# Sums of squares as a rounded part and a remainder, multiplied by ones inside the third column

## The chip, the cores and the metric

The kernel runs on one core of a Trainium2 chip. The metric is the time of one execution on the device in microseconds (us). Engines are named as in the profile: PE is the matmul engine (PEld its weight loads), ACT is ScalarE, DVE is VectorE, POOL is GpSimd, SP issues most transfers.

## The reference

One inference step of a decoder of two layers on 320 tokens (256 of a prompt, 8 x 8 of a batch with a cache), with a width of 1024, all in fp32. Each layer has three sub-layers, and each of them begins with an RMS norm over the width:

```python
def rmsnorm(x, gain):
    xf = x.astype(jnp.float32)
    y = xf * lax.rsqrt(jnp.mean(xf * xf, axis=-1, keepdims=True) + RMS_EPS)
    return (y * gain.astype(jnp.float32)).astype(x.dtype)

x = x + 0.5 * swiglu(rmsnorm(x, ffn1_norm), ffn1_w_gate, ffn1_w_up, ffn1_w_down)
z = rmsnorm(x, mix_norm) @ w_in          # then attention, pooling, convolution, gating
x = x + jnp.concatenate([att, pool, conv, gmlp], axis=-1) @ w_out
x = x + 0.5 * swiglu(rmsnorm(x, ffn2_norm), ffn2_w_gate, ffn2_w_up, ffn2_w_down)
```

The keys, values and states of the mixers are returned too.

## The kernel before

Tokens lie along the free axis (320 columns), features on the 128 partitions. Every large matrix product is made of fp32r matmuls: weights and inputs are each split into a rounded part ("hi") and a remainder ("lo"), and a product is hi x hi + hi x lo + lo x hi, three matmuls for each tile of 128 x 128 weights. The weights stream in through four slots (`raw`, `w_hi`, `w_lo`, index j): SP loads a slot, ACT rounds it (`round_slot`, L971 to L977), POOL subtracts (`split_iteration`, L494 to L501), PE multiplies. In the stages whose input is a norm, a slot is one output column of eight k tiles, 24 matmuls, and its result goes to bank j; an iteration is four columns. Loading waits for the split of the slot's last content, rounding for the transfer (`raw_in`) and for PE to be done with the slot (`slots`), and PE waits for the split (`split`) and for the bank (`taken`).

The norm is applied behind the product: the input enters the product multiplied by its gain alone (`xg_hi`, `xg_lo`), and DVE multiplies what it reads out of a bank by `rms`, the reciprocal of the root of the mean square. The squares are added up on ACT and DVE while the sub-layer before ends (`norm_input`, `add_square`), last into `sumsq`. Then

- PE multiplies `sumsq` by a matrix of ones in fp32 (`sum_squares`, L644 to L647, called at L642 for the first norm of the first layer, behind column 2, and at L677 for the others, ahead of column 2), into bank 6;
- ACT takes the root into `root` (`root_of_norm`, L956 to L958);
- DVE takes the reciprocal into `rms` (`invert_norm`, L1229 to L1232), and only then can read out the banks 0 to 3 of the first iteration (L1241, L1243, L1283), which PE needs free for the next.

All engines work through their own program in order, written out by hand. What stands on ACT around the root decides what waits with it: at the first norm of a layer (`first_step`, L994 to L1005) two slots of the next iteration are rounded ahead of the root and one behind it; at the second (L1076, L1077) the root comes right behind the last squares, and two slots follow; at the third (L1192) four copies of states (L1195, L1197) and a table load follow, and then the slots.

SP, between layers, issues seven small loads (`load_small`, L367 to L377) ahead of the slots of the first stage's second iteration.

Of the kernel before, what the change touches and what calls it, by code (L numbers as in the profile page):

```python
# [24 lines left out]
F32 = mybir.dt.float32  # L25
F32R = mybir.dt.float32r
I32 = mybir.dt.int32
ALU = mybir.AluOpType
ACT = mybir.ActivationFunctionType
AX = mybir.AxisListType  # L30

P = 128
DEPTH, D_MODEL, FFN = 2, 1024, 2816
SEQ, DEC_B, DEC_T = 256, 8, 8
NS = DEC_B * DEC_T
TOK = SEQ + NS
# [5 lines left out]
RMS_EPS, LN_EPS = 1e-6, 1e-5  # L42
SCALE = HEAD ** -0.5
DT = D_MODEL // P
# [55 lines left out]
def hybrid_decoder(nc, xT, w8, w11, gains, vecs, consts, pool_w, conv_pw, sp_wT, sp_b,  # L100
# [3 lines left out]
    with ctx:  # L104
        place = [16512]

        def sb(name, shape, dt=F32, at=None):
            n = 4
            for s in shape[1:]:
                n *= s  # L110
            offset = place[0] if at is None else at[0]
            t = nc.alloc_sbuf_tensor_at(name, shape, dt, offset=offset)
            end = offset + (n + 31) // 32 * 32
            if at is None:
                place[0] = end
                assert end <= 229344, (name, end)
            else:
                at[0] = end
                assert end <= at[1], (name, end, at[1])
            return t  # L120
# [14 lines left out]
        h_lo = sb("h_lo", [P, FT, TOK], F32R)  # L135
        ffn_region[1] = place[0]
        cst = sb("cst", [P, NC_])
        ones = sb("ones", [P, P])
        gain = sb("gain", [P, (3 * DEPTH + 1) * DT])
        vec = sb("vec", [P, DEPTH * NV])  # L140
        page_row = sb("page_row", [1, DEC_B * PAGES], I32)
# [6 lines left out]
        pool_in = sb("pool_in", [P, GT, POOL_HIST + SEQ + DEC_B * (POOL_HIST + DEC_T)])  # L148
        conv_y = sb("conv_y", [P, GT, TOK])
        rms = sb("rms", [P, TOK])  # L150
        root = sb("root", [P, TOK])
        sumsq = sb("sumsq", [P, TOK])
        square = sb("square", [P, 2, TOK])
        tmp = sb("tmp", [P, 8, TOK])
        q_pad = sb("q_pad", [P, GT, DEC_B, 32])
# [58 lines left out]
        def sig(name, per_layer, head=0):  # L214
            return Signal(ctx.enter_context(nc.semaphore(name)), per_layer, head)
# [21 lines left out]
        squared_first = sig("squared_first", 0)  # L237
        squared_too = sig("squared_too", 0)
        summed = sig("summed", 3 * DT, DT)
        norm_sum = sig("norm_sum", 3)  # L240
        norm_root = sig("norm_root", 3)
        norm_ok = sig("norm_ok", 3)
# [102 lines left out]
        def hold(engine, sem, value):  # L345


            engine.wait_ge(sem, value)
            engine.sem_inc(passed.sem, 1)
# [246 lines left out]
        def _(pe):  # L596
# [46 lines left out]

            def sum_squares(L, n):  # L644

                pe.wait_ge(summed.sem, L * summed.per + (n + 1) * DT)
                pe.matmul(bank[6][:, 0:TOK], ones[:, :], sumsq[:, :], start=True, stop=True).then_inc(norm_sum.sem, 1)  # L647

            def column(L, base, tile0, i, j):

                bank_free(L, i * 4 + (tile0 + j))
                use_slot(L, base, i, j, bank[j][:, 0:TOK], range(8), xg_hi, xg_lo, True, True)
# [5 lines left out]
            def open_columns(L, base, tile0, norm):  # L658

                def products(j, k):  # L660
                    hi, lo = w_hi[:, j, k * P:(k + 1) * P], w_lo[:, j, k * P:(k + 1) * P]
                    out = bank[j][:, 0:TOK]
                    pe.matmul(out, hi, xg_hi[:, k, :], start=k == 0, stop=False, skip_group_check=True)  # L663
                    pe.matmul(out, hi, xg_lo[:, k, :], start=False, stop=False, skip_group_check=True)  # L664
                    return pe.matmul(out, lo, xg_hi[:, k, :], start=False, stop=k == DT - 1, skip_group_check=True)  # L665

                for j in range(2):
                    bank_free(L, tile0 + j)
                    pe.wait_ge(split.sem, split.at(L, base * 4 + j + 1))
                    for k in range(DT - 1):  # L670
                        if j == 0:
                            pe.wait_ge(xg_lo_ok.sem, xg_lo_ok.at(L, norm * DT + k + 1 - DT))
                        products(j, k)
                pe.wait_ge(xg_lo_ok.sem, xg_lo_ok.at(L, norm * DT))
                for j in range(2):
                    products(j, DT - 1).then_inc(slots.sem, 1)
                sum_squares(L, norm)  # L677
                for j in range(2, 4):
                    column(L, base, tile0, 0, j)

            def down(L, base, tile0, ffn):
                with pe.Fori(0, IT_D // 2) as i2:
# [83 lines left out]
            def conv_mean(L):  # L766
                pe.wait_ge(taps.sem, taps.at(L, taps.per))
                pe.wait_ge(late_taps.sem, late_taps.at(L, late_taps.per))
                for c in range(GT):
                    mm = pe.matmul(bank[7][:, 0:TOK], ones[:, :], conv_y[:, c, :], start=c == 0, stop=c == 1)  # L770
                mm.then_inc(cv_mean.sem, 1)

            def conv_variance(L):
                pe.wait_ge(cv_sq.sem, cv_sq.at(L, 2))
                for c in range(GT):
                    mm = pe.matmul(bank[7][:, 0:TOK], ones[:, :], conv_sq[:, c, :], start=c == 0, stop=c == 1)
                mm.then_inc(cv_var.sem, 1)

            def prompt_attention_transposes(L):
# [173 lines left out]
        def _(act):  # L953
            act.sem_inc(states_out.sem, 16)

            def root_of_norm(L, n):  # L956
                act.wait_ge(norm_sum.sem, norm_sum.at(L, n + 1))
                act.activation(root[:, :], bank[6][:, 0:TOK], ACT.Sqrt, bias=eps_rms, scale=1.0 / D_MODEL).then_inc(norm_root.sem, 1)  # L958

            def round_input(gain_col, d):  # L960

# [9 lines left out]
            def round_slot(L, base, i, j, halves):  # L971

                count = halves[j][1]
                act.wait_ge(raw_in[j].sem, L * raw_in[j].per + (base + i) * 16 + 16)

                act.wait_ge(slots.sem, L * slots.per + (base + i) * 4 + j + 1)
                act.activation(w_hi[:, j, 0:count * P], raw[:, j, 0:count * P], ACT.Copy).then_inc(split_hi.sem, 1)  # L977
# [16 lines left out]
            def first_step(L):  # L994

                round_slot(L, BASE_G1, 1, 0, HALVES8)
                round_slot(L, BASE_G1, 1, 1, HALVES8)
                root_of_norm(L, 0)
                round_slot(L, BASE_G1, 1, 2, HALVES8)
                act.preload_act_table(ACT.Silu)  # L1000
                silu(L, 0, 0, T_G1)
                round_slot(L, BASE_G1, 1, 3, HALVES8)
                round_h(L, 0, 0, 0)
                silu(L, 0, 1, T_G1)
                round_h(L, 0, 1, 0)  # L1005
# [15 lines left out]
            def norm_tile(L, tile0, norm, d, e):  # L1021
                hold(act, taken.sem, L * taken.per + d + (tile0 + 1 + taken.head))
                norm_input(L * (3 * DT) + d + norm * DT, d, e, L * summed.per + d + (norm * DT - 1))

            def down(L, base, tile0, norm, last):

                def step(i, e):
                    for j in range(4):
                        round_slot(L, base, i + 1, j, HALVES11)
                    norm_tile(L, tile0, norm, i, e)  # L1030

                act.preload_act_table(ACT.Sqrt)
                with act.Fori(0, DT // 2 - 1) as i2:
                    for e in range(2):
                        step(i2 * 2 + e, e)
                step(DT - 2, 0)
                for j in range(4):
                    if last:
                        round_slot(L + 1, BASE_G1, 0, j, HALVES8)
                    else:  # L1040
                        round_slot(L, BASE_I, 0, j, HALVES8)
                norm_tile(L, tile0, norm, DT - 1, 1)
# [30 lines left out]
            with act.Fori(0, DEPTH) as L:  # L1073
                first_step(L)
                gate_up(L, BASE_G1, T_G1, 0, 1)
                down(L, BASE_D1, T_D1, 1, False)  # L1076
                root_of_norm(L, 1)  # L1077

                def sigmoid(c):
# [107 lines left out]
                for i in range(IT_O):  # L1187
                    for j in range(4):
                        base_next, i_next = ((BASE_O, 1), (BASE_G2, 0))[i]
                        round_slot(L, base_next, i_next, j, HALVES8)  # L1190
                        norm_tile(L, T_O, 2, 4 * i + j, j % 2)
                root_of_norm(L, 2)  # L1192
                for c in range(GT):
                    _, rows = split_tokens(conv_in[:, c, :], CONV_HIST + DEC_T, CONV_HIST)
# [7 lines left out]
        @block.vector  # L1202
        def _(dve):
            dve.sem_inc(taken.sem, 4)
            for n, (ap, value) in enumerate(((stat[:, 42:43], 1.0), (stat[:, 60:61], RMS_EPS), (stat[:, 61:62], LN_EPS), (ones[:, :], 1.0), (q_pad[:, :, :, :], 0.0),
                                             (conv_in[:, :, 0:CONV_HIST], 0.0), (pool_in[:, :, 0:POOL_HIST], 0.0))):
                last = dve.memset(ap, value)
            last.then_inc(filled.sem, 1)
# [18 lines left out]
                    dve.tensor_tensor(sumsq[:, :] if d == DT - 1 else square_sum, square_sum, squares, ALU.add).then_inc(summed.sem, 1)  # L1227

            def invert_norm(L, n):  # L1229
                dve.wait_ge(norm_root.sem, norm_root.at(L, n + 1))  # L1230
                dve.reciprocal(rms[:, :], root[:, :]).then_inc(norm_ok.sem, 1)
                hold(dve, norm_ok.sem, norm_ok.at(L, n + 1))  # L1232

            def gate_up_step(L, base, tile0, ffn, i):
# [401 lines left out]
```

## Time and profile before

| | us |
|---|---|
| time, median of 3 | 1172.51 (1172.4 to 1175.3) |
| the profiled execution | 1173.95 |
| its span | 1172.1 |
| PE busy in it | 1152.9 (98%) |
| POOL busy | 815.1 (70%) |
| DVE busy | 635.4 (54%) |
| ACT busy | 545.5 (47%) |

The profile is of one execution. Times in its rows count from the span's start. A row of the order in time begins with the start and the length in us; "x8" stands for eight instructions in a row, and a bracket tells how long the engine had been idle and what released it. Matmuls overlap, so the length of one is more than the distance to the next.

### The profile page before, as it was taken

The numbers are of one execution on the slowest core, as the hardware profiler recorded it, in microseconds if no ns is written. First come the engines' busy times: TensorE is split into PE (matmuls) and PEld (weight loads), VectorE is DVE, ScalarE is ACT, GpSimd is POOL, SyncE is SP. The second block draws the span as 40 slices with busy tenths as digits, with TensorE's granted clock in tenths as the row PEclk, the third lists the DMA queues.
The fourth block names the chain that finished last, engine by engine and source line by source line (L and its number), as shares of the span: only waits on it lengthen the run. The fifth ranks groups of instructions, "written<-read, shape, count | busy, mean of one in ns | idle before, by whom it ended". The sixth has DMA issues, their size and how long they took to land.

```text
span 1172.1 us, 23918 instructions
## 1 busy us (share of the span) xinstructions
PE 1152.9 (98%) x7912; PEld 1132.8 (97%) x7912; DVE 635.4 (54%) x894; ACT 545.5 (47%) x822; POOL 815.1 (70%) x425
## 2 busy tenths in 40 slices
PE   7999999999999999999999999999999999999998
PEld 6999999998899999999999999999987999999998
DVE  5777762249856544432247776622597664444222
ACT  5444444444665444444444444444357654444444
POOL 5776667777766766667767777677686776666677
PEclk9999999999999999999999999999999999999999
DMA  8454435556535544445564444455563654444455
GB/s 289 154 161 145 154 107 151 147 177 192 173 112 165 176 144 154 140 122 148 169 183 161 144 145 150 122 148 168 179 183 121 173 156 153 156 148 125 138 150 170
DMA packets 72795, 183.14 MB, mean 156 GB/s; under 512 B 10274, under 2 KB 25890, under 8 KB 72738
## 3 DMA queue, kind: packets, MB, share of 16 engines
q1 hardware_dynamic: 72256, 181.33, 50.8%
q10 hardware_dynamic: 482, 1.16, 0.3%
q8 instruction: 23, 0.38, 0.1%
q14 instruction: 34, 0.28, 0.1%
HBM read 178.88 MB, written 3.58 MB: 156 GB/s over the span
## 4 chain that ended last, share of the span: by engine, by line
PE 45%; POOL 25%; issue 24%; DVE 2%; DMA 1%; POOLq 1%; SPq 1%; DVEq 1%; ACT 0%; ACTq 0%
POOL w_lo L500 24%; PE bank L604 13%; PE bank L605 13%; PE bank L607 13%; DVE bank L1292 1%; PE bank L886 1%; PE bank L888 1%; PE bank L887 1%; POOL win L532 1%; DMA x<-in_xT 1%; DMA raw<-in_w 1%; PE bank L664 0%; PE bank L665 0%; PE bank L663 0%; POOLq L499 0%
## 5 line engine op out<-in xcount | busy, mean ns | idle before, releaser
L500 POOL TENSOR_TENSOR w_lo<-raw,w_hi 128x1024 fp32r<-128x1024 f32 (+2 forms) x355 | 776.0, 2192 | 331.2 <-ACT w_hi L977 330.9
L977 ACT ACTIVATE w_hi<-raw 128x1024 fp32r<-128x1024 f32 (+2 forms) x355 | 340.6, 961 | 410.1 <-PE bank L607 388.2
L604 PE MATMUL bank<-xg_hi,w_hi 128*128 128x320 f32 x1552 | 482.2, 311 | 4.0 <-DVE tmp L1241 2.0
L607 PE MATMUL bank<-xg_hi,w_lo 128*128 128x320 f32 x1552 | 479.5, 309 | 0.0
L605 PE MATMUL bank<-xg_lo,w_hi 128*128 128x320 f32 x1552 | 479.5, 309 | 0.0
L604 PEld LDWEIGHTS bank<-xg_hi,w_hi 128*128 128x128 f32 x1552 | 291.3, 188 | 8.0 <-issue 4.6
L605 PEld LDWEIGHTS bank<-xg_lo,w_hi 128*128 128x128 f32 x1552 | 291.3, 188 | 0.4
L607 PEld LDWEIGHTS bank<-xg_hi,w_lo 128*128 128x128 f32 x1552 | 291.3, 188 | 0.0
L604 PE MATMUL bank<-h_hi,w_hi 128*128 128x320 f32 x704 | 217.5, 309 | 0.0
L605 PE MATMUL bank<-h_lo,w_hi 128*128 128x320 f32 x704 | 217.5, 309 | 0.0
L607 PE MATMUL bank<-h_hi,w_lo 128*128 128x320 f32 x704 | 217.5, 309 | 0.0
L1248 DVE TENSOR_TENSOR h_lo<-tmp,h_hi 128x320 f32 (+1 forms) x88 | 169.8, 1930 | 73.4 <-ACT h_hi L991 73.4
L1265 DVE SCALAR_TENSOR_TENSOR x<-bank,x 128x320 f32<-128x320 f32 x48 | 23.4, 486 | 201.1 <-PE bank L607 198.6
L604 PEld LDWEIGHTS bank<-h_hi,w_hi 128*128 128x128 f32 x704 | 132.1, 188 | 0.0
L605 PEld LDWEIGHTS bank<-h_lo,w_hi 128*128 128x128 f32 x704 | 132.1, 188 | 0.0
L607 PEld LDWEIGHTS bank<-h_hi,w_lo 128*128 128x128 f32 x704 | 132.1, 188 | 0.0
L1243 DVE TENSOR_TENSOR tmp<-bank,rms 128x320 f32<-128x320 f32 x88 | 42.9, 487 | 130.4 <-PE bank L607 130.2
L1215 DVE SCALAR_TENSOR_TENSOR xg_lo<-x,gain,xg_hi 128x320 fp32r<-128x320 f32 x56 | 72.3, 1299 | 56.8 <-ACT xg_hi L962 56.8
L987 ACT ACTIVATE tmp<-tmp 128x320 f32<-128x320 f32 x88 | 40.9, 465 | 91.9 <-DVE tmp L1241 91.7
L1246 DVE TENSOR_TENSOR tmp<-tmp 128x320 f32<-128x320 f32 x88 | 62.2, 707 | 9.5 <-ACT tmp L987 7.2
L1320 DVE SCALAR_TENSOR_TENSOR conv_y<-conv_in,vec,conv_y 128x64 f32<-128x64 f32 x88 | 62.7, 753 | 2.8
L991 ACT ACTIVATE h_hi<-tmp 128x320 f32 (+1 forms) x88 | 41.2, 469 | 28.9 <-DVE tmp L1246 28.9
(187 smaller groups left out, 846.2 us busy)
## 6 DMA issues: line engine op xcount, KB each, us to landing
raw<-in_w SPq DMA_DIRECT2D x227, 512.0 KB, 3.9
raw<-in_w SPq DMA_DIRECT2D x64, 384.0 KB, 3.1
raw<-in_w SPq DMA_DIRECT2D x64, 320.0 KB, 2.9
k_all<-in_cache_kT SPq DMA_DIRECT2D x32, 128.0 KB, 3.1
v_past<-in_cache_v SPq DMA_DIRECT2D x32, 128.0 KB, 2.8
cst<-in_consts ACTq DMA_DIRECT2D x1, 997.0 KB
out_yT<-x SPq DMA_DIRECT2D x1, 960.0 KB, 5.9
x<-in_xT SPq DMA_DIRECT2D x2, 320.0 KB, 4.0
```

The source lines that it names most:

```text
L500: pool.tensor_tensor(w_lo[:, j, 0:count * P], raw[:, j, 0:count * P], w_hi[:, j, 0:count * P].bitcast(F32), ALU.subtract).then_inc(split.s ...
L604: pe.matmul(out, hi, in_hi[:, k, :], start=first and n == 0, stop=False)
L605: pe.matmul(out, hi, in_lo[:, k, :], start=False, stop=False)
L607: mm = pe.matmul(out, lo, in_hi[:, k, :], start=False, stop=last and end)
L977: act.activation(w_hi[:, j, 0:count * P], raw[:, j, 0:count * P], ACT.Copy).then_inc(split_hi.sem, 1)
L987: act.activation(tmp[:, 2 + m, :], tmp[:, m, :], ACT.Silu).then_inc(silu_ok.sem, 1)
L991: act.activation(h_hi[:, bass.ds(i * 2 + m, 1), :].rearrange("p a t -> p (a t)"), tmp[:, 6 + m, :], ACT.Copy).then_inc(h_hi_ok.sem, 1)
L1215: dve.scalar_tensor_tensor(out=xg_lo[:, bass.ds(d, 1), :].rearrange("p a t -> p (a t)"), in0=one, scalar=gain[:, bass.ds(gain_col, 1)], in ...
L1243: dve.tensor_tensor(tmp[:, 4 + m, :], bank[2 * m + 1][:, 0:TOK], rms[:, :], ALU.mult).then_inc(taken.sem, 1)
L1246: dve.tensor_tensor(tmp[:, 6 + m, :], tmp[:, 2 + m, :], tmp[:, 4 + m, :], ALU.mult).then_inc(h_ok.sem, 1)
L1248: dve.tensor_tensor(h_lo[:, bass.ds(i * 2 + m, 1), :].rearrange("p a t -> p (a t)"), tmp[:, 6 + m, :], h_hi[:, bass.ds(i * 2 + m, 1), :].b ...
L1320: dve.scalar_tensor_tensor(out=y, in0=window, scalar=weight, in1=y, op0=ALU.mult, op1=ALU.add).then_inc(batch_taps.sem, 1)
```

## The change

The matrix of ones becomes fp32r (the same bytes are still read as fp32 by the convolution's two sums). ACT rounds `sumsq` into `sum_hi` (`round_sum`, right ahead of each root), DVE subtracts to give `sum_lo` (at the head of `invert_norm`), and PE multiplies both by the ones, in two fp32r matmuls into bank 6, after a wait for the remainder. In `open_columns` this moves from ahead of column 2 to the middle of it, behind its fourth k tile; in `first_columns` its place stays. The root is written over the sum in bank 6, and the reciprocal reads it there.

```diff
@@ allocation, signals
-        ones = sb("ones", [P, P])
+        ones_r = sb("ones_r", [P, P], F32R)
+        ones = ones_r[:, :].bitcast(F32)
-        root = sb("root", [P, TOK])
+        sum_hi = sb("sum_hi", [P, TOK], F32R)
+        sum_lo = sb("sum_lo", [P, TOK], F32R)
+        sum_hi_ok = sig("sum_hi_ok", 3)
+        sum_lo_ok = sig("sum_lo_ok", 3)
@@ PE
             def sum_squares(L, n):
-                pe.wait_ge(summed.sem, L * summed.per + (n + 1) * DT)
-                pe.matmul(bank[6][:, 0:TOK], ones[:, :], sumsq[:, :], start=True, stop=True).then_inc(norm_sum.sem, 1)
+                pe.wait_ge(sum_lo_ok.sem, sum_lo_ok.at(L, n + 1))
+                pe.matmul(bank[6][:, 0:TOK], ones_r[:, :], sum_hi[:, :], start=True, stop=False, skip_group_check=True)
+                pe.matmul(bank[6][:, 0:TOK], ones_r[:, :], sum_lo[:, :], start=False, stop=True, skip_group_check=True).then_inc(norm_sum.sem, 1)
@@ PE, open_columns
-                sum_squares(L, norm)
-                for j in range(2, 4):
-                    column(L, base, tile0, 0, j)
+                bank_free(L, tile0 + 2)
+                pe.wait_ge(split.sem, split.at(L, base * 4 + 3))
+                for k in range(DT):
+                    if k == DT // 2:
+                        sum_squares(L, norm)
+                    mm = products(2, k)
+                mm.then_inc(slots.sem, 1)
+                column(L, base, tile0, 0, 3)
@@ ACT
+            def round_sum(L, n):
+                hold(act, summed.sem, L * summed.per + (n + 1) * DT)
+                act.activation(sum_hi[:, :], sumsq[:, :], ACT.Copy).then_inc(sum_hi_ok.sem, 1)
...
-                act.activation(root[:, :], bank[6][:, 0:TOK], ACT.Sqrt, bias=eps_rms, scale=1.0 / D_MODEL).then_inc(norm_root.sem, 1)
+                act.activation(bank[6][:, 0:TOK], bank[6][:, 0:TOK], ACT.Sqrt, bias=eps_rms, scale=1.0 / D_MODEL).then_inc(norm_root.sem, 1)
...
                 round_slot(L, BASE_G1, 1, 0, HALVES8)
                 round_slot(L, BASE_G1, 1, 1, HALVES8)
+                round_sum(L, 0)
                 root_of_norm(L, 0)
...
+                round_sum(L, 1)
                 root_of_norm(L, 1)
...
+                round_sum(L, 2)
                 root_of_norm(L, 2)
@@ DVE
             def invert_norm(L, n):
+                dve.wait_ge(sum_hi_ok.sem, sum_hi_ok.at(L, n + 1))
+                dve.tensor_tensor(sum_lo[:, :], sumsq[:, :], sum_hi[:, :].bitcast(F32), ALU.subtract).then_inc(sum_lo_ok.sem, 1)
                 dve.wait_ge(norm_root.sem, norm_root.at(L, n + 1))
-                dve.reciprocal(rms[:, :], root[:, :]).then_inc(norm_ok.sem, 1)
+                dve.reciprocal(rms[:, :], bank[6][:, 0:TOK]).then_inc(norm_ok.sem, 1)
```

## Rows read from the trace of the kernel before

**Rows 1.** The page: busy us, share of the span and instructions of each engine.

```profile
PE 1152.9 (98%) x7912; PEld 1132.8 (97%) x7912; DVE 635.4 (54%) x894; ACT 545.5 (47%) x822; POOL 815.1 (70%) x425
```

**Rows 2.** Order in time around the first norm: start, length, engine, instruction, count, idle before.

```profile
17.11 1.34 PE L625 MATMUL bank<-xg_lo,w_hi 128*128 128x320 f32 x8
22.98 0.70 PE L647 MATMUL bank<-sumsq,ones 128*128 128x320 f32 x2
23.01 1.06 ACT L977 ACTIVATE w_hi<-raw 128x1024 fp32r<-128x1024 f32 x1 [3.18 <-DMA raw<-in_w]
23.97 0.51 ACT L958 ACTIVATE root<-bank,stat 128x320 f32<-128x320 f32 x1
24.37 2.41 POOL L500 TENSOR_TENSOR w_lo<-raw,w_hi 128x1024 fp32r<-128x1024 f32 x1
24.51 2.15 DVE L1231 RECIPROCAL rms<-root 128x320 f32<-128x320 f32 x1 [4.46 <-ACT root L958]
24.68 1.34 PE L625 MATMUL bank<-xg_lo,w_hi 128*128 128x320 f32 x8
27.54 0.41 PE L604 MATMUL bank<-xg_hi,w_hi 128*128 128x320 f32 x1 [0.34 <-DVE tmp L1241]
```

**Rows 3.** DVE's subtractions (line L1248: ns min/median/max), and one beside POOL in time.

```profile
L1248 DVE TENSOR_TENSOR h_lo<-tmp,h_hi x88: 492/2028/2326, 30.1 to 1091.7; 128x320 f32 x84, 128x320 fp32r<-128x320 f32 x4
...
606.94 2.58 POOL L500 TENSOR_TENSOR w_lo<-raw,w_hi 128x1024 fp32r<-128x1024 f32 x1
607.87 2.00 DVE L1248 TENSOR_TENSOR h_lo<-tmp,h_hi 128x320 fp32r<-128x320 f32 x1 [0.62 <-ACT h_hi L991]
```

**Rows 4.** Order in time around the first norm of the second layer.

```profile
596.18 0.70 PE L647 MATMUL bank<-sumsq,ones 128*128 128x320 f32 x2
601.03 1.06 ACT L977 ACTIVATE w_hi<-raw 128x1024 fp32r<-128x1024 f32 x1 [2.18 <-DMA raw<-in_w]
601.99 0.51 ACT L958 ACTIVATE root<-bank,stat 128x320 f32<-128x320 f32 x1
602.16 2.40 POOL L500 TENSOR_TENSOR w_lo<-raw,w_hi 128x1024 fp32r<-128x1024 f32 x1 [0.83 <-ACT w_hi L977]
605.55 0.41 PE L604 MATMUL bank<-xg_hi,w_hi 128*128 128x320 f32 x1 [1.62 <-DVE tmp L1241]
```

**Rows 5.** Order in time around the second norm of the first layer.

```profile
250.24 0.48 DVE L1227 TENSOR_TENSOR sumsq<-bank,square 128x320 f32<-128x320 f32 x1
252.91 0.70 PE L647 MATMUL bank<-sumsq,ones 128*128 128x320 f32 x2
253.65 0.53 ACT L958 ACTIVATE root<-bank,stat 128x320 f32<-128x320 f32 x1 [5.71 <-PE bank L647]
255.20 2.42 POOL L500 TENSOR_TENSOR w_lo<-raw,w_hi 128x1024 fp32r<-128x1024 f32 x1 [5.23 <-ACT w_hi L977]
```

**Rows 6.** Order in time behind the third norm of the first layer.

```profile
366.89 1.06 ACT L977 ACTIVATE w_hi<-raw 128x1024 fp32r<-128x1024 f32 x1
368.03 2.42 POOL L500 TENSOR_TENSOR w_lo<-raw,w_hi 128x1024 fp32r<-128x1024 f32 x1 [7.99 <-ACT w_hi L977]
370.90 0.31 PE L604 MATMUL bank<-xg_hi,w_hi 128*128 128x320 f32 x1
```

**Rows 7.** PE's first matmuls in order of time.

```profile
8.64 1.27 PE L625 MATMUL bank<-xg_lo,w_hi 128*128 128x320 f32 x4
9.71 1.27 PE L629 MATMUL bank<-xg_hi,w_lo 128*128 128x320 f32 x4
11.47 1.99 PE L621 MATMUL bank<-xg_hi,w_hi 128*128 128x320 f32 x4 [0.49 <-ACT xg_hi L962]
15.39 1.88 PE L621 MATMUL bank<-xg_hi,w_hi 128*128 128x320 f32 x8
```

**Rows 8.** Stretches: length, busy us (instructions) by engine, granted clock, DMA share, GB/s.

```profile
0.00:6.50 6.50, 0.00 (x0) 0.01 (x1) 1.89 (x9) 2.93 (x4) 0.25 (x5) 1.00 0.62 168
6.50:16.60 10.10, 9.22 (x29) 7.78 (x30) 5.96 (x11) 7.84 (x14) 4.58 (x3) 1.00 1.03 385
```

More of the change, by code:

```diff
@@ L769, in conv_mean @@
                 for c in range(GT):
-                    mm = pe.matmul(bank[7][:, 0:TOK], ones[:, :], conv_y[:, c, :], start=c == 0, stop=c == 1)
+                    mm = pe.matmul(bank[7][:, 0:TOK], ones, conv_y[:, c, :], start=c == 0, stop=c == 1)
                 mm.then_inc(cv_mean.sem, 1)
@@ L775, in conv_variance @@
                 for c in range(GT):
-                    mm = pe.matmul(bank[7][:, 0:TOK], ones[:, :], conv_sq[:, c, :], start=c == 0, stop=c == 1)
+                    mm = pe.matmul(bank[7][:, 0:TOK], ones, conv_sq[:, c, :], start=c == 0, stop=c == 1)
                 mm.then_inc(cv_var.sem, 1)
@@ L1204, in _ @@
             dve.sem_inc(taken.sem, 4)
-            for n, (ap, value) in enumerate(((stat[:, 42:43], 1.0), (stat[:, 60:61], RMS_EPS), (stat[:, 61:62], LN_EPS), (ones[:, :], 1.0), (q_pad[:, :, :, :], 0.0),
+            for n, (ap, value) in enumerate(((stat[:, 42:43], 1.0), (stat[:, 60:61], RMS_EPS), (stat[:, 61:62], LN_EPS), (ones, 1.0), (q_pad[:, :, :, :], 0.0),
                                              (conv_in[:, :, 0:CONV_HIST], 0.0), (pool_in[:, :, 0:POOL_HIST], 0.0))):
```

## Prediction

> **What bounds the kernel now.** I read the busy table first: the matmul engine (PE) is busy 98% of the span, the next engine (POOL) 70% [rows 1]. A kernel like this ends later by each gap that opens in the PE stream, and earlier by each matmul taken out of it; work elsewhere counts only where it makes PE wait. So I looked at PE's own order in time, around the six sums of squares (three norms in each of two layers), and beside it at what ScalarE (ACT), VectorE (DVE) and POOL do there. The unit of all that follows is the distance of two matmul starts, 128x128 on 320 columns: from 17.11 us, the second third of column 1, to the sum at 22.98 there are 40 of them (16 left of column 1, 24 of column 2), so 5.87/40 = 0.147 us each [rows 2]. A column is 24 of them, 3.52 us.
>
> **What the change takes away.** A sum is two records [rows 2]. From its start at 22.98 to the second third of the next column at 24.68 lie 1.70 us, of which eight matmuls are 1.18, so the fp32 sum costs PE 0.52 us [rows 2]. Two fp32r matmuls of the same shape cost 0.29. The change takes 0.23 us from PE at each norm, 1.4 us in all. The trace shows no fp32r matmul against a constant matrix; the kernel's other fp32r matmuls are the nearest rows. If the pair still ran like fp32, a sum would cost 1.04 and the six norms 3.1 us more than now instead of 1.4 less.
>
> **What it adds.** Ahead of the pair stand a copy on ACT (128x320, about 0.47 us, like the root's 0.51) and a subtraction on DVE with both operands in SBUF. The same kind of subtraction in this kernel takes 0.49 us when POOL is idle, but 2.03 at the median [rows 3]: the one at 607.87 ended at 609.87, 0.35 us after the POOL subtraction that ran from 606.94 to 609.52 [rows 3]. I take from this that it lands 0.35 us after the end of the POOL instruction that it finds running, and 0.49 after its start where POOL is idle. PE now waits for its result, and all that is queued on PE behind that wait (the rest of the third column, the fourth, and what follows) waits with it. The root comes after the pair: before, it began 0.74 us after the sum's start (252.91 to 253.65) [rows 5]; the pair is 0.24 shorter, so 0.50. The root in PSUM and the reciprocal that reads it there are in no row; DVE's and ACT's rows with an operand in PSUM (0.51 for the root, which reads it) bound them to some 0.1 us either way, and I take nothing.
>
> **First norm, layer 0: +3.7 us.** This sum stands after the whole third column, the change doesn't move it. PE arrives at 22.98 [rows 2]. But ACT, in the order of its program, rounds slot 1 of the next iteration before it comes to the new copy, and that waits for a weight transfer until 23.01; the root, next in line, began at 23.97 [rows 2]. The copy takes that place: 23.97 to 24.44. The subtraction reaches DVE at 24.48, 0.11 us after a POOL instruction began, 24.37 to 26.78 [rows 2], and lands at 27.13. PE starts the pair at S = 27.2, idle for 4.1 us. Now the chain behind: the root at S + 0.50, the reciprocal 0.54 later (23.97 to 24.51), and the next iteration's first column, for which bank 0 must be read out, 3.03 later (24.51 to 27.54) [rows 2]: 31.27. PE itself, with 26 matmuls, is done at S + 3.82 = 31.0, so the bank is last. It was 27.54: +3.7.
>
> **First norm, layer 1: +5.0 us.** Here the pair stands after the fourth of the eight k tiles of column 2. Without the sum that now lies at 596.18, PE gets there at 596.18 + 12 x 0.147 = 597.94. ACT again has two slots to round first; the second waits 2.18 us for its transfer and starts at 601.03, the root behind it at 601.99 [rows 4]. Nothing of this hurt before: PE had the sum done long ago and two columns to go. Now the copy takes the root's place, 601.99 to 602.46; POOL begins its subtraction at 602.16 and ends at 604.56 [rows 4], so the remainder lands at 604.91 and S = 604.98. PE idles 7.0 us. After it come 2 + 12 + 24 matmuls, 5.59 us, to 610.57; the chain through the root would allow 609.05, and slots 0 and 1 have both been split by 604.56, so nothing else is late. It was 605.55, with 1.62 us of idle before it that the new stall swallows [rows 4]: +5.0.
>
> **Second norm, both layers: -0.5 us.** The sum of squares starts at 250.24 and takes 0.48, ACT and DVE then stand idle and POOL does until 255.20 [rows 5]; the copy and the remainder are done by 251.9. PE comes at 252.91 + 1.76 = 254.67 and doesn't wait. The root slides by 1.76 - 0.24 = 1.52 us, and with it POOL's first split of the next iteration, to 256.72 to 259.14. It is needed after 50 matmuls, at 260.2, so it stays covered by 1.1 us. The saving stands: 2 x 0.23.
>
> **Third norm, both layers: +2.4 us.** Again PE doesn't wait for the remainder, and again ACT slides by 1.52 us. But here it has four copies and a table load between root and slot: rounding starts at 366.89, POOL runs from 368.03 to 370.45, and PE takes the slot at 370.90 [rows 6], a cover of 0.45 us only. POOL will end at 371.97, and PE, 0.1 us later, start at 372.1: +1.2 in each layer. The bounds are -0.23 (all covered) and +1.5 (the whole slide). The slots behind have a column, 3.52 us, each against 2.42 on POOL, and catch up.
>
> **Sum at full matmul rate:** 3.7 + 5.0 - 0.5 + 2.4 = 10.6 us.
>
> **What the idle does to the matmul rate.** In the first 16 us matmuls start 0.267 us apart (four from 8.64 to 9.71 [rows 7]), which is 320 columns at 1.2 GHz, though the granted clock reads 1.00 over that stretch [rows 8]. The eight from 15.39 to 17.11 take 1.72 us, so the change to 0.147 (the 2.4 GHz level) falls near 16.6, some 5.1 us after the last gap, 0.49 us before 11.47 [rows 7]. PE had nothing in the first 6.5 us [rows 8]. Since no later gap of PE is over 1.62 us [rows 4], the trace doesn't show whether one of 4.1 or 7.0 us brings the slow rate back. If it does, 5.1 us at 0.267 are 19 matmuls, which would take 2.8: a loss of 2.3 us; nothing at the low end, and taken from the first matmuls on (6.5 to 16.6) 10.1 us, of which 45% (0.12 of each 0.267) is 4.5. I take it that the gap of 7.0 us is enough, as it is about the 6.5 us that stood before the first matmul, and that of 4.1 us not: +2.3.
> The Trainium skill (TensorE: Matmul & The Clock Gate, "Why this matters for your kernels") warns of idle gaps between bursts of matmuls, since an idle matmul engine falls back to half rate; by that rule both stalls would bring the slow rate back, which is the first rival below.
>
> **Forecast.** 10.6 + 2.3 = 12.9 us. The profiled execution took 1173.95 us with a span of 1172.1, 1.4 over the median of 1172.51; the deltas are differences inside the span, and I add them to the median: 1185.4 us.
>
> **Rivals.**
> Both stalls bring the slow rate back: the first one's 2.3 us are covered for 0.25 by the bank's chain, so +2.0, 1187.4 us. For it: the start of the trace. Against: the gap is shorter than the one seen there.
> Neither does: 1183.1 us. For it: the granted clock read full even while the matmuls were slow [rows 8], so nothing in the trace ties the slow rate to a gap.
> The remainder of layer 0 slips in before the POOL instruction. It misses it by 0.11 us; if it came first, S would be 25.05, the next column 29.1, and that norm +1.6 instead of 3.7: 1183.3 us.
> The other side: the copy is in time. If the two slots of the first norms were rounded about 1.05 us (copy 0.47, remainder 0.49, hops) ahead of PE's arrival, that is if ACT got to the copy by 21.9 and 596.9, and the third norm's cover held, only the savings would stay: 1172.5 - 1.4 = 1171.1 us. Against it: transfers that land at 23.0 and 601.0, and nothing in the change makes them earlier.
>
> **Chances.** Forecast 0.42; both slow 0.23; neither slow 0.15; slipped in 0.10; in time 0.05; something else 0.05, of which pairs as dear as fp32 (4.5 us more) are one. The range runs from 1180.5 (neither slow, the third norm nearly covered) to 1189.5 (both slow, and the slow stretch longer). A measurement tells 0.3%, 3.5 us, from no change: slower by that is 0.93, within it 0.05 (the case in time), faster 0.02.
>
> **What would show it.** In the profile after: PE idle some 4 and 7 us before the sum's two matmuls in the first norms, with the remainder as releaser; remainders of about 2.4 us there and 0.5 elsewhere; a wait of about 1.2 us for the weights' low part in the third norms; two records of 0.31 us for each sum. Matmuls 0.267 apart behind the long gap show the clock's share. I am wrong if the first norms show no gap, or if what PE loses there is won back before the end.

## The result, and the profile after

| | before | after |
|---|---|---|
| time, median (lowest to highest), us | 1172.52 (1172.4 to 1175.3) | 1196.13 (1194.86 to 1197.51) |
| span of the profiled execution, us | 1172.1 | 1194.3 |
| mean granted clock in it | 0.999 | 0.989 |

The ratio is 1.0199, with a 95% interval of 1.0187 to 1.0210: slower by 23.6 us, where 12.9 were forecast and 1189.5 was the upper end of the range.

The page of after, first its busy line, to be held against [rows 1]:

```profile
PE 1158.4 (97%) x7912; PEld 1138.8 (95%) x7912; DVE 641.7 (54%) x900; ACT 549.2 (46%) x828; POOL 812.4 (68%) x425
```

PE's instructions are as many as before (two records a sum, in both). ACT and DVE are busy for 3.7 and 6.3 us more, and PE for 5.5, which no added instruction explains. What PE waited for, and where it ran slowly, does. The waits of PE in after, longest sum first (us in total, times, longest):

```profile
PE bank L651 <- DVE sum_lo L1248: 10.9, 2, 6.2
PE bank L608 <- issue: 8.2, 2, 4.1
PE bank L625 <- ACT w_hi L997: 6.6, 1, 6.6
PE bank L608 <- POOL w_lo L504: 2.3, 2, 1.1
```

and the same view of before:

```profile
PE bank L621 <- ACT w_hi L983: 6.5, 1, 6.5
PE bank L604 <- DVE tmp L1241: 2.0, 2, 1.6
PE bank L604 <- issue: 1.5, 2, 0.8
...
PE bank L604 <- POOL w_lo L500: 0.5, 2, 0.2
```

PE's first wait is the same (6.6 and 6.5). The waits for the remainder (10.9) and for the weights' low part (2.3) are those of the forecast. The waits of 4.1 us with no releaser shown ("issue"), one in each layer, are not in it.

Where the time went can be read more exactly: both kernels run the same 7900 matmuls apart from the sums, in the same order, so each start in after can be set against its partner in before. The difference, stretch by stretch, worked out from the two traces and read where it stays constant for hundreds of matmuls, behind each norm or the mixers:

| stretch | layer 0, us | layer 1, us | forecast, us |
|---|---|---|---|
| first norm (in layer 0 with the program's start) | +4.9 | +6.4 | +3.7, +7.3 (2.3 of it the slow rate) |
| second norm and the mixers behind it | +3.9 | +4.7 | -0.23 each |
| third norm | +1.2 | +1.1 | +1.2 each |

These sum to 22.2, the difference of the spans; the medians differ by 23.6, since the profiled execution of before was 1.4 over its median. First and third norms come to 13.6 against 13.4 forecast. The second norms take 8.6 where a gain was expected. (The expectations of the experiments below give some of these differences 0.1 to 0.2 us higher or lower.)

Order in time around the first norm of layer 0 in after, for [rows 2] (start, length, engine, instruction, idle before and its releaser):

```profile
22.23 1.06 ACT L991 ACTIVATE w_hi<-raw 128x1024 fp32r<-128x1024 f32 x1 [3.21 <-DMA raw<-in_w]
23.20 0.45 ACT L968 ACTIVATE sum_hi<-sumsq 128x320 fp32r<-128x320 f32 x1
23.68 2.48 DVE L1248 TENSOR_TENSOR sum_lo<-sumsq,sum_hi 128x320 fp32r<-128x320 f32 x1 [4.50 <-ACT sum_hi L968]
26.22 0.64 PE L651 MATMUL bank<-sum_hi,ones_r 128*128 128x320 f32 x1 [4.73 <-DVE sum_lo L1248]
27.16 0.50 ACT L972 ACTIVATE bank<-bank,stat 128x320 f32<-128x320 f32 x1 [3.51 <-PE bank L652]
27.69 2.16 DVE L1250 RECIPROCAL rms<-bank 128x320 f32<-128x320 f32 x1 [1.53 <-ACT bank L972]
32.57 0.31 PE L608 MATMUL bank<-xg_hi,w_hi 128*128 128x320 f32 x1
```

The chain is the forecast's: a transfer, the slot, the copy in the root's old place, a remainder of 2.48 us beside POOL, PE idle for 4.73 us. PE was done with column 2 some 1.6 us earlier than in before, where its last eight matmuls began at 21.81 against 20.16 here: its starts were 0.147 apart by 12.2 us here, and only from 16.6 on in before. The wait, whose end a transfer sets, took that up again. The root in PSUM takes 0.50 and its reciprocal 2.16, against 0.51 and 2.15 [rows 2]. But from the pair at 26.22 to the next column at 32.57 are 6.35 us, where 26 matmuls at 0.147 would be 3.82 and the bank's chain 4.07. The first norm of layer 1, for [rows 4]:

```profile
611.38 0.45 ACT L968 ACTIVATE sum_hi<-sumsq 128x320 fp32r<-128x320 f32 x1
611.87 2.37 DVE L1248 TENSOR_TENSOR sum_lo<-sumsq,sum_hi 128x320 fp32r<-128x320 f32 x1 [7.93 <-ACT sum_hi L968]
614.30 0.64 PE L651 MATMUL bank<-sum_hi,ones_r 128*128 128x320 f32 x1 [6.22 <-DVE sum_lo L1248]
614.99 0.47 PE L668 MATMUL bank<-xg_hi,w_hi 128*128 128x320 f32 x1
615.26 0.47 PE L669 MATMUL bank<-xg_lo,w_hi 128*128 128x320 f32 x1
```

Behind the gap the starts lie 0.27 us apart (614.99 to 615.26). The stretches behind the three kinds of gap, and one behind a short gap (length, busy us and instructions of PE, PEld, DVE, ACT, POOL, granted clock, DMA share, GB/s):

```profile
26.20:32.50 6.30, 6.28 (x26) 6.28 (x27) 3.54 (x4) 3.22 (x4) 2.37 (x1) 0.57 0.43 134
283.52:288.00 4.48, 4.48 (x20) 4.48 (x21) 4.48 (x12) 3.97 (x6) 2.98 (x3) 0.62 0.01 3
614.30:618.70 4.40, 4.40 (x16) 4.40 (x17) 2.69 (x3) 0.77 (x2) 0.00 (x0) 0.50 0.43 130
380.78:384.30 3.52, 3.52 (x24) 3.52 (x25) 2.67 (x4) 1.60 (x3) 3.52 (x2) 1.00 0.51 153
```

After 4.73, 4.10 and 6.22 us of idle the granted clock is near one half, the 1.2 GHz level, and the matmuls' starts lie nearly twice as far apart. After the 1.15 us of the third norm it is 1.00, and 24 matmuls take 3.52 as ever. Behind the gap of 6.22 us the starts are back to 0.147 apart from about 618.7 on.

Last the second norm, the stretch that the forecast had wrong. In before, DVE and POOL at the mixers' first products (the gates of the convolution, four products of which L1357 and L1358 take two each):

```profile
261.10 1.56 DVE L1357 TENSOR_TENSOR conv_in<-tmp 128x256 f32<-128x256 f32 x1
262.58 0.21 DVE L1358 TENSOR_TENSOR conv_in<-tmp 128x64 f32<-128x64 f32 x1
262.71 0.41 DVE L1357 TENSOR_TENSOR conv_in<-tmp 128x256 f32<-128x256 f32 x1
263.05 2.44 DVE L1358 TENSOR_TENSOR conv_in<-tmp 128x64 f32<-128x64 f32 x1
...
255.20 7.17 POOL L500 TENSOR_TENSOR w_lo<-raw,w_hi 128x1024 fp32r<-128x1024 f32 x3 [5.23 <-ACT w_hi L977]
262.71 5.06 POOL L500 TENSOR_TENSOR w_lo<-raw,w_hi 128x1024 fp32r<-128x1024 f32 x2 [0.34 <-ACT w_hi L977]
```

and in after:

```profile
265.79 0.94 DVE L1376 TENSOR_TENSOR conv_in<-tmp 128x256 f32<-128x256 f32 x1
266.65 2.44 DVE L1377 TENSOR_TENSOR conv_in<-tmp 128x64 f32<-128x64 f32 x1
269.01 2.65 DVE L1376 TENSOR_TENSOR conv_in<-tmp 128x256 f32<-128x256 f32 x1
271.58 2.43 DVE L1377 TENSOR_TENSOR conv_in<-tmp 128x64 f32<-128x64 f32 x1
...
282.94 1.28 DVE L1302 TENSOR_TENSOR qk<-bank,rms 128x320 f32<-128x320 f32 x3
...
261.65 12.28 POOL L504 TENSOR_TENSOR w_lo<-raw,w_hi 128x1024 fp32r<-128x1024 f32 x5 [6.77 <-ACT w_hi L991]
...
283.52 0.39 PE L608 MATMUL bank<-xg_hi,w_hi 128*128 128x320 f32 x1 [4.10 <-issue]
```

Both operands of these products lie in SBUF. In before the first product waits for the subtraction that ends at 262.37; POOL then waits for a slot for 0.34 us, two more products pass at 0.21 and 0.41 us, and the last waits for POOL again. In after the five subtractions run as one row, and three products take about as long as a subtraction each. The four last 8.2 us instead of 4.4 (265.79 to 274.01, 261.10 to 265.49). Behind them in DVE's program stand 22 steps of the convolution and then the read-outs of q and k, on which PE waits for its banks: 282.94 in after, and PE 0.58 later.

### The profile page after: what moved, and what is told of

It reads as the page before. It is cut to its first block, busy times and chain, and to the rows that moved or that the text cites. A ratio compares the mean times of both kernels' runs of the same rounds, so it can differ in the third digit from the quotient of the medians.

```text
span 1194.3 us, 23942 instructions
## 1 busy us (share of the span) xinstructions
PE 1158.4 (97%) x7912; PEld 1138.8 (95%) x7912; DVE 641.7 (54%) x900; ACT 549.2 (46%) x828; POOL 812.4 (68%) x425
## 4 chain that ended last, share of the span: by engine, by line
PE 58%; issue 19%; POOL 17%; DMA 2%; DVE 1%; POOLq 1%; SPq 1%; ACT 0%; DVEq 0%; ACTq 0%
PE bank L611 19%; PE bank L609 19%; PE bank L608 19%; POOL w_lo L504 14%; POOL win L536 1%; DMA raw<-in_w 1%; PE bank L668 1%; PE bank L670 1%; PE bank L669 1%; DMA x<-in_xT 1%; DVE conv_in L1376 1%; POOL tmp L520 1%; DVE conv_in L1377 0%; DVE sum_lo L1248 0%; SPq L381 0%
## 5 line engine op out<-in xcount | busy, mean ns | idle before, releaser
L608 PE MATMUL bank<-xg_hi,w_hi 128*128 128x320 f32 x1512 | 470.5, 311 | 10.5 <-issue 8.2
L609 PE MATMUL bank<-xg_lo,w_hi 128*128 128x320 f32 x1512 | 469.1, 310 | 0.0
L611 PE MATMUL bank<-xg_hi,w_lo 128*128 128x320 f32 x1512 | 468.9, 310 | 0.0
L608 PEld LDWEIGHTS bank<-xg_hi,w_hi 128*128 128x128 f32 x1512 | 285.6, 189 | 13.6 <-issue 8.6
L609 PEld LDWEIGHTS bank<-xg_lo,w_hi 128*128 128x128 f32 x1512 | 285.6, 189 | 0.0
L611 PEld LDWEIGHTS bank<-xg_hi,w_lo 128*128 128x128 f32 x1512 | 285.5, 189 | 0.0
L1265 DVE TENSOR_TENSOR tmp<-tmp 128x320 f32<-128x320 f32 x88 | 60.1, 683 | 10.9 <-ACT tmp L1001 8.6
L1339 DVE SCALAR_TENSOR_TENSOR conv_y<-conv_in,vec,conv_y 128x64 f32<-128x64 f32 x88 | 55.7, 673 | 2.9
```

Source lines behind the costliest of these rows:

```text
L608: pe.matmul(out, hi, in_hi[:, k, :], start=first and n == 0, stop=False)
L609: pe.matmul(out, hi, in_lo[:, k, :], start=False, stop=False)
L611: mm = pe.matmul(out, lo, in_hi[:, k, :], start=False, stop=last and end)
L1265: dve.tensor_tensor(tmp[:, 6 + m, :], tmp[:, 2 + m, :], tmp[:, 4 + m, :], ALU.mult).then_inc(h_ok.sem, 1)
L1339: dve.scalar_tensor_tensor(out=y, in0=window, scalar=weight, in1=y, op0=ALU.mult, op1=ALU.add).then_inc(batch_taps.sem, 1)
```

## The experiments

The theory, from the comparison of the traces: there are two chains. One is the forecast's, the pair that waits for a late remainder, with the slow rate behind it. The other is that the sum in the middle of the column makes root and slots late, that POOL's row then has no gap, and that DVE's products stall behind it. The rival: the mixers' stall is no chain of its own but follows from the first norms' delay or from the rounding, and a kernel without either has none. Every kernel below was compared with the kernel before in the same session; changes in microseconds are against that median (1172.08 for the first four, 1172.72 for the others).

### The copy ahead of the slots, at the first norms

```diff
+                round_sum(L, 0)
                 round_slot(L, BASE_G1, 1, 0, HALVES8)
                 round_slot(L, BASE_G1, 1, 1, HALVES8)
-                round_sum(L, 0)
                 root_of_norm(L, 0)
```

> The changed kernel with the copy of the first norms (both layers) moved on ScalarE ahead of the two slots that it stood behind; the root stays behind them. Theory (the first norms cost what the copy's late place costs): in the changed kernel the first norms add 5.0 us (layer 0) and 6.6 us (layer 1) to the matmul stream; here both fall to about 0, so 1196.1 - 11.6 = 1184.5 us, no gap ahead of the sums' matmuls, and no slow matmuls behind them. Rival (the wait for the remainder is late whatever stands ahead of it, since the subtraction must wait for GpSimd): still some 2.5 us at each first norm, 1189 to 1190 us.

Measured: 1184.28, ratio 1.0098 [1.0081, 1.0115], so 12.2 us over before, where after is 23.6 over. PE's waits:

```profile
PE bank L608 <- issue: 8.2, 2, 4.1
...
PE bank L608 <- POOL w_lo L504: 2.3, 2, 1.1
```

The wait for the remainder is gone and the two others stand as in after. The first norms' share hangs on the copy's place on ACT alone, and the rest has another cause.

### The second norm's pair ahead of column 2

```diff
-                    if k == DT // 2:
+                    if k == (0 if norm == 1 else DT // 2):
                         sum_squares(L, norm)
```

> The changed kernel with the pair of the second norms (both layers) ahead of column 2 instead of in its middle. Theory (the second norms cost 3.7 and 4.9 us because the root came 1.5 us later there): the cost goes, the saving of 0.23 each stays: 1196.1 - 9.1 = 1187.0 us, and the wait of 4.1 us that the matmul engine shows in the mixer stage is gone. Rival (the cost comes from the pair, the copy or the remainder themselves, or from the root in PSUM): unchanged, 1196 us.

Measured: 1186.31, ratio 1.0122 [1.0105, 1.0139]. The waits named "issue" fall from 8.2 to 0.5 us in total, while the first norms' remain:

```profile
PE bank L651 <- DVE sum_lo L1248: 9.4, 2, 4.7
...
PE bank L608 <- issue: 0.5, 2, 0.2
```

So the mixers' stall belongs to the move by half a column at the second norm, not to the rounding there.

### The gates in PSUM

The sum stays in the middle of the column; the sigmoid writes the gates to banks 4 and 5, so that each product has one operand only in SBUF.

```diff
-                    act.activation(z_g[:, c, :], z_g[:, c, :], ACT.Sigmoid).then_inc(glu_sig.sem, 1)
+                    act.activation(bank[4 + c][:, 0:TOK], z_g[:, c, :], ACT.Sigmoid).then_inc(glu_sig.sem, 1)
...
-                    dve.tensor_tensor(conv_in[:, c, CONV_HIST:CONV_HIST + SEQ], z_a[:, c, 0:SEQ], z_g[:, c, 0:SEQ], ALU.mult).then_inc(glu_ok.sem, 1)
-                    dve.tensor_tensor(history(c)[:, :, CONV_HIST:], batch(z_a[:, c, SEQ:TOK]), batch(z_g[:, c, SEQ:TOK]), ALU.mult).then_inc(glu_ok.sem, 1)
+                    dve.tensor_tensor(conv_in[:, c, CONV_HIST:CONV_HIST + SEQ], z_a[:, c, 0:SEQ], bank[4 + c][:, 0:SEQ], ALU.mult).then_inc(glu_ok.sem, 1)
+                    dve.tensor_tensor(history(c)[:, :, CONV_HIST:], batch(z_a[:, c, SEQ:TOK]), batch(bank[4 + c][:, SEQ:TOK]), ALU.mult).then_inc(glu_ok.sem, 1)
```

> The changed kernel with the sigmoids of the gates written to PSUM (banks 4 and 5) instead of SBUF, so that the four products behind the second norm read one SBUF operand, not two; the root is as late as in the changed kernel. Theory (the late root shifted these products under an unbroken row of GpSimd subtractions, and each waits for one of them to end): the products take 0.2 to 0.5 us each instead of 0.9 to 2.7, the wait in the mixer stage goes, and with it the wait of 0.8 us that the kernel before has there: 1196.1 - 9.1 - 1.5 = 1185.5 us. Rival (lateness alone: the 1.5 us of the root pass on to the matmul engine): the wait stays above 1 us each, 1193 to 1196 us.

Measured: 1183.60, ratio 1.0092 [1.0075, 1.0109]. DVE and POOL, order in time:

```profile
266.19 0.41 DVE L1376 TENSOR_TENSOR conv_in<-tmp,bank 128x256 f32<-128x256 f32 x1
266.51 0.21 DVE L1377 TENSOR_TENSOR conv_in<-tmp,bank 128x64 f32<-128x64 f32 x1
266.78 0.42 DVE L1376 TENSOR_TENSOR conv_in<-tmp,bank 128x256 f32<-128x256 f32 x1
267.12 0.21 DVE L1377 TENSOR_TENSOR conv_in<-tmp,bank 128x64 f32<-128x64 f32 x1
...
262.05 11.92 POOL L504 TENSOR_TENSOR w_lo<-raw,w_hi 128x1024 fp32r<-128x1024 f32 x5 [6.77 <-ACT w_hi L991]
```

POOL's row is as unbroken as in after, the root as late, and yet the four products take 1.1 us and the mixers' wait is gone. This tells the late root from what it acts through: it is the products behind POOL that cost the time. By the matmuls' starts the stretch is now 2.0 us shorter than in before, in each layer, more than the wait of 0.8 us that before has there and the pair's saving make up: the products cost time in before too.
The Trainium skill (SBUF — State Buffer, "SBUF: two separate sides") says that a DVE operation with two SBUF inputs and a GpSimd operation exclude each other, for the whole of an instruction; these rows agree, 0.21 us with one input in SBUF against 2.44 with two.

### Useless matmuls in the wait

PE multiplies 26 (layer 0) or 40 (layer 1) times into a bank that is free, ahead of the wait at the first norms. This adds work only.

```diff
+                if n == 0:
+                    for f in range(40 if L else 26):
+                        pe.matmul(bank[5][:, 0:TOK], w_hi[:, 2, f % DT * P:(f % DT + 1) * P], xg_hi[:, f % DT, :], start=True, stop=True, skip_group_check=True)
                 pe.wait_ge(sum_lo_ok.sem, sum_lo_ok.at(L, n + 1))
```

> The changed kernel with 26 (layer 0) and 40 (layer 1) matmuls of no use put ahead of the wait for the remainder in the first norms, of the form of the others and into an unused bank, so that the matmul engine idles under 1 us there while everything else stays. Theory (the idle itself brings the slow rate back, and costs some 2.3 us at the first and 2.0 us at the second of them beside the idle): matmuls behind the sums 0.147 us apart, granted clock 1.0 there, 1196.1 - 4.3 = 1191.8 us. Rival (the rate falls for another reason than the idle): matmuls still 0.267 apart behind the sums, 1196 us or more.

Measured: 1192.77, ratio 1.0175 [1.0158, 1.0192], 20.7 us over before where after is 23.6. The stretches of the table above:

```profile
26.20:32.50 6.30, 5.71 (x37) 5.45 (x38) 4.00 (x5) 4.49 (x6) 2.74 (x3) 1.00 0.40 142
614.30:622.00 7.70, 7.70 (x55) 7.70 (x54) 5.47 (x5) 4.24 (x5) 4.66 (x2) 1.00 0.31 110
```

and, in order of time, the pair and the next column in layer 0, then the remainder and the pair in layer 1:

```profile
26.71 0.42 PE L654 MATMUL bank<-sum_hi,ones_r 128*128 128x320 f32 x1 [1.01 <-DVE sum_lo L1251]
30.88 0.41 PE L608 MATMUL bank<-xg_hi,w_hi 128*128 128x320 f32 x1
609.59 0.56 DVE L1251 TENSOR_TENSOR sum_lo<-sumsq,sum_hi 128x320 fp32r<-128x320 f32 x1 [6.59 <-ACT sum_hi L971]
612.85 0.31 PE L654 MATMUL bank<-sum_hi,ones_r 128*128 128x320 f32 x1
```

The granted clock is 1.00 in both stretches. In layer 0 the pair starts no earlier than in after (26.71 against 26.22). In layer 1 the second slot's transfer came earlier in this execution, the remainder took 0.56 us and was there at 610.15, and the pair stood behind the useless matmuls until 612.85; so this norm shows the rate without the idle, but not the wait. From the pair to the next column are 4.17 us (layer 0) and 5.56 us (layer 1, from 612.85 to 618.41), where after has 6.35 and 7.67. So the slow rate at the first norms is caused by the idle before it, and is worth 2.2 and 2.1 us there, close to the 4.3 us expected; the medians moved by 2.9, as the useless matmuls cost time too. The waits of 8.1 us at the mixers are untouched.

### The move alone, and the rounding alone

The move alone is the kernel before, its fp32 sum in the middle of column 2 and nothing else changed:

```diff
-                sum_squares(L, norm)
-                for j in range(2, 4):
-                    column(L, base, tile0, 0, j)
+                bank_free(L, tile0 + 2)
+                pe.wait_ge(split.sem, split.at(L, base * 4 + 3))
+                for k in range(DT):
+                    if k == DT // 2:
+                        sum_squares(L, norm)
+                    mm = products(2, k)
+                mm.then_inc(slots.sem, 1)
+                column(L, base, tile0, 0, 3)
```

> The kernel before with one part of the change alone: the fp32 sum moved into the middle of column 2 in the five later norms, no rounding, no remainder. Theory (the second and third norms pay for the move, the first for the rounding): nothing at the first norms; at the second the wait of some 4 us in the mixer stage and slow matmuls behind it, 9.6 us in both layers; at the third some 2.8 us: 1172.1 + 12.4 = 1184.5 us. Rival (the new instructions shift DVE and GpSimd against each other, the move is harmless): 1172 to 1174 us.

Measured: 1185.60, ratio 1.0113 [1.0098, 1.0129], +12.9. Its waits:

```profile
PE bank L604 <- issue: 9.2, 2, 4.6
...
PE bank L604 <- POOL w_lo L500: 2.3, 2, 1.1
```

The rounding alone is the kernel after, with every pair ahead of column 2:

```diff
-                    if k == DT // 2:
+                    if k == 0:
                         sum_squares(L, norm)
```

> The changed kernel without the move: rounding, remainder and pair as changed, but the pair ahead of column 2 in all later norms. Theory: the second and third norms save 0.23 us each and nothing waits there; the first norms pay, 5.0 us in layer 0 as in the changed kernel, and in layer 1 some 8.3 us (6.6 as in the changed kernel, and 1.8 more since the matmul engine comes to the wait 12 matmuls earlier): 1172.1 + 5.0 + 8.3 - 0.9 = 1184.5 us. Rival (the middle of column 2 is what hurts at every norm): below 1178 us.

Measured: 1184.96, ratio 1.0108 [1.0092, 1.0123], +12.2. Its waits:

```profile
PE bank L651 <- DVE sum_lo L1248: 11.7, 2, 7.6
...
PE bank L608 <- issue: 0.5, 2, 0.3
PE bank L608 <- POOL w_lo L504: 0.5, 2, 0.2
```

The two halves of the change cost about the same, by different chains: the move hurts second and third norms and no first one, the rounding hurts the first norms and no other. Together they are 25.1 us, against 23.6 for the whole change; the excess of 1.5 us lies within the intervals of these medians. Set start against start, the move alone adds 5.0 and 5.3 us at the second norms and 1.4 at each third one, and the rounding alone 4.9 and 8.4 at the first norms, while it takes 0.2 to 0.6 off each of the others.

### Copy and root early, and the gates too

If that is all, the rounded pair itself should gain what the forecast gave it. Copy and root go ahead of both slots at the first norms, and every pair ahead of column 2:

```diff
-                round_slot(L, BASE_G1, 1, 0, HALVES8)
-                round_slot(L, BASE_G1, 1, 1, HALVES8)
                 round_sum(L, 0)
                 root_of_norm(L, 0)
+                round_slot(L, BASE_G1, 1, 0, HALVES8)
+                round_slot(L, BASE_G1, 1, 1, HALVES8)
...
-                    if k == DT // 2:
+                    if k == 0:
```

> The changed kernel with the copy and the root of the first norms both ahead of the two slots on ScalarE, and the pair ahead of column 2 (before its first k tile) in all five places where it stood in the middle. Theory (what the change cost came from the two places alone, and the rounded pair itself saves 0.23 us a norm): no waits for the remainder, none in the mixer stage, none for the weights' low part; the wait of 1.6 us that the kernel before has behind the first norm of layer 1 goes too, since the root no longer stands behind the second transfer, and some 0.4 us of the one in layer 0: -0.9 - 2.0 - 0.5 = -3.4, near 1168.7 us. Rival (the pair, copy and remainder have a cost of their own): 1172 us or more.

Measured: 1169.50 (1168.82 to 1169.96), ratio 0.9973 [0.9964, 0.9982]. PE has no wait for the remainder, and none for a read-out at the next iteration's first column. Two waits that were expected to go are smaller or still there: 0.5 us in the mixers and 1.0 us for the weights' low part, each in total. Of 3.2 us gained, the pairs are 1.4 by the forecast's price, and most of the rest lies where before waited 1.62 us for a read-out [rows 4]. At the third norms the shift of PE's starts against before is -0.24 and -0.25 us, close to the pair's saving of 0.23 in the forecast.

The same with the gates in PSUM (the edit shown above):

> The kernel of the run before in this list (copy and root first, pair ahead of column 2) with the gates' sigmoids in PSUM as well. Theory (the products behind the second norm lose time to GpSimd's subtractions in the kernel before too, where the matmul engine waits 0.8 and 0.7 us in the mixer stage): -3.4 - 1.5 = -4.9, near 1167.2 us. Rival (that wait has another cause): as the run without it, 1168.7 us.

Measured: 1166.63 (1166.50 to 1167.79), ratio 0.9956 [0.9942, 0.9969]: faster than both kernels, by 6.1 and 29.5 us. The gates are worth 2.9 us here where 1.5 were expected; the starts put 1.4 of it in the mixers of each layer, at the read-outs of q and k and behind them. Which waits of before make up the surplus was not followed further.

## Why the prediction was wrong

**The direction and the mechanism of the first norms were right.** PE idles 4.73 and 6.22 us there (4.1 and 7.0 forecast), with the remainder as releaser, 2.48 and 2.37 us long. In layer 0 the pair started at 26.22, not 27.2, mostly because the transfer ahead of it came 0.8 us earlier in this execution; the slow rate, which the forecast did not give this norm, then took 2.3 us more than 4.07. In layer 1 there were 0.8 us less of idle than forecast, and 2.1 of slow rate against 2.3.

**The slow rate: the likeliest case was wrongly chosen.** I let only the gap of 7.0 us bring it back, because the one at the program's start was 6.5 long, and counted the full granted clock [rows 8] as evidence against. That 1.00 was no reading: the trace of before holds no record of the granted clock ahead of 16.61 us, and the stretch view prints 1.00 where there is none. Its first record begins where the starts come to be 0.147 apart. Gaps of 4.10 and 4.73 us did it too, and the granted clock then read 0.62 and 0.57. The rival with both stalls slow was right on this, at 1187.4, and still 8.7 us short.
The Trainium skill as cited in the prediction (TensorE: Matmul & The Clock Gate, "Why this matters for your kernels") says that an idle matmul engine falls back to half rate; after agrees at all four of its long gaps, of 4.07 to 6.22 us, with a granted clock of 0.50 to 0.62 behind them.

**The second norms: the step that failed.** "It stays covered by 1.1 us" followed the late root from ACT to POOL to PE's next slots, and that part was right: no wait for a slot shows there. It did not ask what else is on POOL's and DVE's programs in those microseconds. Four products with both operands in SBUF are, and their price was in the rows that the prediction itself used for DVE's subtractions: such an operation that meets a POOL instruction lands 0.35 us after its end [rows 3]. Applied to the four products it gives one POOL instruction, some 2.4 us, for each. The move of 1.5 us closed the one gap in POOL's row in which three of them had ended or passed in before. The 3.8 us lost there on DVE come out at the read-outs of q and k as a wait of 4.1 us instead of 0.8, and the idle brings the slow rate back, another 1.1 us (layer 0) and 1.9 us (layer 1) by the shift of the starts behind it. Measured: +3.9 and +4.7 us instead of -0.23 each. With the pair ahead of the column, or with the gates in PSUM, the wait is gone; with the move alone, it is there. How the gap closes is an observation of these traces and not a separate experiment: POOL's row started later, and ACT had its slots rounded by the time POOL came to them.

**The third norms were right.** POOL releases PE after 1.15 us in both layers, and the shifts there are +1.2 and +1.1, against +1.2. With the pair ahead of the column the wait falls to 0.5 in total.

**The small terms were right.** The pair's matmuls start 0.147 us apart where PE runs on, root and reciprocal cost nothing more in PSUM, and the remainders off POOL take 0.49 us. The saving itself shows in the version with everything early, 0.24 and 0.25 us at the third norms.

In the sum: 13.4 forecast for first and third norms, 13.6 measured; -0.5 for the second, 8.6 measured. That the first two numbers agree so well is partly luck: the first norm of layer 0 came out 1.2 over its forecast and that of layer 1 0.9 under, since an earlier transfer hid part of the slow rate that layer 0 had not been given. The range ended at 1189.5 because it held bounds only for steps that I had looked at; the second norm had been given none.

## What to carry to other kernels

When an edit makes one instruction of a chain later, follow every engine that its followers share something with, and not only the chain to the bottleneck: here the harm went from POOL to DVE without any semaphore between them, and showed at PE some 18 us later as a wait without a releaser. A DVE operation with two operands in SBUF beside a busy POOL should be priced at one POOL instruction, each; moving one operand to PSUM made it independent of POOL. And a copy added to a chain belongs on its engine ahead of whatever waits for a transfer, not in the place of the step that it prepares.

## What the runs showed of the hardware

- A gap of 4.1 us in PE's stream was followed by 0.267 us between matmuls (320 columns at 1.2 GHz) and a granted clock of 0.62; one of 1.15 us was not (1.00, and 0.147). No run has a gap of PE between 1.62 [rows 4] and 4.07 us. The length of the last gap does not decide alone: at the program's start, where PE had run slowly, the version with the copy first went fast and then slow again, behind no gap over 0.77 us (two stretches, in the form of those above):

```profile
12.80:13.70 0.90, 0.90 (x7) 0.80 (x7) 0.90 (x3) 0.90 (x3) 0.00 (x0) 1.00 1.10 376
13.80:17.10 3.30, 3.30 (x14) 3.17 (x13) 3.17 (x4) 2.28 (x3) 2.84 (x2) 0.50 1.08 414
```

- The granted clock showed the slow level in the middle of the program (0.50 from 614.30 to 618.70). At the program's start, where matmuls were as far apart, it printed 1.00 [rows 7, 8] for want of a record: the records begin at 16.61 us in before and at 11.17 in after. Until the first record the distance of the starts is the one to read.
- Four small DVE products took 8.2 us behind an unbroken row of POOL subtractions, 4.4 where the row had a gap of 0.34 us, and 1.1 with one operand in PSUM.
